# Three and six token tiles instead of four and five, 52 and 44 hosted expert groups, another order in the joint attention stage, and weights laid out by slice

## What is computed

```
a = rmsnorm(h, norm_mix)
z = a @ w_in                                  # 1024 x 9240
y_m = sigmoid(o) * mlstm_chunkwise(...)       # 4 heads of 256, a recurrent state
y_f = fox_attention(...)                      # 16 heads of 64, causal, with forget gates
h = h + (sig(g_m) * (y_m @ w_br_m) + sig(g_f) * (y_f @ w_br_f)) @ w_out
# PEER: 8 heads pick 16 experts each of 16384, by two top-16 lists of 128 keys
act = gelu(einsum('thkd,td->thk', u_tab[idx], x))
h = h + einsum('thk,thkd->td', g * act, v_tab[idx])
h = h + sigmoid(rmsnorm(h) @ w_ple_gate) * (p @ w_ple_proj)
```

## Time and profile before

| what | value |
|---|---|
| time, median of three runs | 5291.07 us (5285.33 to 5294.82) |
| the profiled execution's own time | 5289.55 us |
| its span | 5287.7 us |
| mean granted TensorE clock | 0.905 of full speed |
| TensorE, VectorE, ScalarE, GpSimd busy | 86%, 58%, 18%, 23% of the span |
| DMA | 1478.71 MB, mean 280 GB/s |

### The profile page before, as it was taken

One profiled execution on the slowest core, in us unless ns is written; L12 is line 12 of the kernel. 1 busy time (PEld: TensorE's weight loads), 2 busy tenths in 40 slices (PEclk: granted clock), 3 DMA queues, 4 the chain that ended last, 5 costly groups with the idle time before them and its releaser, 6 DMA issues. The chain is left out here.

```text
span 5287.7 us, 47730 instructions
## 1 busy us (share of the span) xinstructions
PE 4532.9 (86%) x16510; PEld 2777.6 (53%) x16510; DVE 3088.6 (58%) x6265; ACT 965.1 (18%) x1797; POOL 1233.2 (23%) x970
## 2 busy tenths in 40 slices
PE   8999669979859999677787689946899999999989
PEld 5555445536535555356566455635455445545444
DVE  1000333214567677489888617589677777777742
ACT  1110321111100111144444311113100000000013
POOL 0000001200004444243343100000344444444410
PEclk9999878889979999777776699969999999999999
DMA  4332344467729999888888687735899999999951
GB/s 143 124 113 87 103 132 152 166 232 285 255 111 392 408 407 402 315 329 317 308 332 313 243 318 276 250 122 171 355 419 419 418 414 417 412 414 415 408 233 58
DMA packets 464418, 1478.71 MB, mean 280 GB/s; under 512 B 38146, under 2 KB 204850, under 8 KB 361298
## 3 DMA queue, kind: packets, MB, share of 16 engines
q0 software_dynamic: 119872, 824.76, 38.7%
q1 hardware_dynamic: 344338, 651.36, 34.3%
HBM read 1370.05 MB, written 115.38 MB: 281 GB/s over the span
## 5 line engine op out<-in xcount | busy, mean ns | idle before, releaser
L2252 POOL DMA_INDIRECT ex_uv<-in_uv,idx x768 | 1142.2, 1487 | 1898.0 <-DVE ex_acc L2309 1646.0
L2293 DVE CUSTOM_DVE_ANT_0 ex_uv<-ex_uv,ex_xp 128x1024 f32<-128x1024 f32 x768 | 915.4, 1221 | 350.3 <-DMA ex_uv<-in_uv,idx 304.7
L2309 DVE SCALAR_TENSOR_TENSOR ex_acc<-ex_uv,ex_wt,ex_acc 128x1024 f32<-128x1024 f32 x768 | 942.2, 1280 | 6.3
L2599 PE MATMUL exp_psum_dn<-exp_dn_big,exp_dn_gg 128*128 128x512 f32 x1536 | 683.4, 595 | 28.1 <-DVE exp_dn_gg L2521 28.1
L2590 PE MATMUL exp_psum_dn<-exp_dn_xT,exp_dn_big 128*128 128x384 f32 x2048 | 684.0, 488 | 13.3 <-DMA exp_dn_big<-in_ud 13.3
L386 PE MATMUL proj_psum_acc<-proj_w,aT_later 128*128 128x385 f32 x1920 | 624.8, 487 | 71.0 <-DMA proj_w<-in_w_in 64.3
L2590 PEld LDWEIGHTS exp_psum_dn<-exp_dn_xT,exp_dn_big 128*128 128x128 f32 x2048 | 390.4, 191 | 313.3 <-issue 62.4
L386 PEld LDWEIGHTS proj_psum_acc<-proj_w,aT_later 128*128 128x128 f32 x1920 | 363.9, 190 | 331.5 <-DMA proj_w<-in_w_in 64.5
L297 PE MATMUL proj_psum_acc<-proj_w,aT 128*128 128x385 f32 x1536 | 501.7, 488 | 5.0 <-DVE aT L230 2.8
L2599 PEld LDWEIGHTS exp_psum_dn<-exp_dn_big,exp_dn_gg 128*128 128x128 f32 x1536 | 290.4, 190 | 377.5 <-issue 350.8
L297 PEld LDWEIGHTS proj_psum_acc<-proj_w,aT 128*128 128x128 f32 x1536 | 291.0, 190 | 211.8 <-issue 4.4
(11 more groups left out here) (363 smaller groups left out, 4560.4 us busy)
## 6 DMA issues: line engine op xcount, KB each, us to landing
proj_w<-in_w_in SPq DMA_DIRECT2D x48, 1540.0 KB, 36.3
rt_w<-in_w_q SPq DMA_DIRECT2D x36, 2048.0 KB, 8.2
exp_dn_big<-in_ud SPq DMA_DIRECT2D x128, 512.0 KB
exp_dn_big<-in_vd SPq DMA_DIRECT2D x128, 512.0 KB, 8.1
scratch_z<-proj_zs SPq DMA_DIRECT2D x216, 192.5 KB, 2.2
rt_w<-in_w_br_m SPq DMA_DIRECT2D x18, 2048.0 KB, 10.0
rt_w<-in_w_br_f SPq DMA_DIRECT2D x18, 2048.0 KB
rt_w<-in_w_out SPq DMA_DIRECT2D x18, 2048.0 KB, 8.9
```

What stands on the lines that cost most here:

```text
L2252: pool.indirect_dma_start(self.uv[:, slot, :], None, self.uv_tab, bass.IndirectOffsetOnAxis(ap=self.idx[:, at:at + 1], axis=0)).then_inc(s ...
L2293: dve.tensor_tensor_reduce(self.uv[:, slot, 0:D], self.uv[:, slot, 0:D], self.xp[:], 1.0, 0.0, ALU.mult, ALU.add, self.dot[:, g % 2, j:j + ...
L2309: dve.scalar_tensor_tensor(out=self.acc[:, j % 2, :], in0=self.uv[:, slot, D:2 * D], scalar=self.wt[:, g % 2, j:j + 1], in1=self.acc[:, j ...
L2599: mm = pe.matmul(self.banks[t][:, n * 512:(n + 1) * 512], self.gg[:, 4 + q % 4, t * P:(t + 1) * P], self.big[:, 4 + q % 4, n * 512:(n + 1) ...
```

## The change

`FIRST` goes from 4 to 3 and `EARLY` from 44 to 52. So the front stage and the first routing handle three tiles, the first attention two blocks, and the second part handles six tiles and six blocks (3 to 8). The projection hosts 52 groups and the joint stage 44. In `stage_attend` ScalarE copies the turned probabilities of the step before ahead of the exponential, and VectorE scales the rows of the step before the last directly behind the maximum. The weights `w_in`, `w_br_m`, `w_br_f`, `w_out` and `w_q` are laid out on the host so that what one load brings stands contiguously for each partition. Some small buffers share memory.

```diff
-FIRST = 4
+FIRST = 3
 HOSTED = 3
-EARLY = 44
+EARLY = 52
...
-                sp.dma_start(w[:, u % U], w_in_v[:, :, u * CW:(u + 1) * CW]).then_inc(w_in_u[u % U], 16)
+                sp.dma_start(w[:, u % U].rearrange("p k n -> p (k n)"), w_in[u]).then_inc(w_in_u[u % U], 16)
...
-                if j + 3 * nt in rides:
+                if rides.get(j + 3 * nt, 0) >= nm.XB:
                     nm.sp_load(sp, rides[j + 3 * nt])
...
-        self.SBUFS = 1024 // self.W if self.W <= 512 else 1
+        self.SBUFS = 2 if self.W <= 512 else 1
...
                     for hd, g in fx.heads_at(s):
                         fx.act_head(act, hd, g)
-                    fx.act_exp(act, s)
                     ml.act_slot(act, *slot(s, 0))
                 if s >= 1:
                     for r in range(fx.rounds(s - 1)):
                         fx.act_probs(act, s - 1, r)
+                if s < STEPS:
+                    fx.act_exp(act, s)
                 for g, unit in hosted(s, 0):
                     ex.act_unit(act, g, unit)
...
-            for s in range(STEPS + 1):
+            for s in range(STEPS + 2):
                 if s < STEPS:
                     fx.dve_max(dve, s)
+                if s >= 2:
+                    fx.dve_y(dve, s - 2)
+                if s < STEPS:
                     ml.dve_slot(dve, *slot(s, 0))
                 for g, unit in hosted(s, 0):
                     ex.dve_unit(dve, g, unit)
                 if s < STEPS:
                     ml.dve_slot(dve, *slot(s, 1))
-                if s >= 1:
-                    fx.dve_y(dve, s - 1)
...
-        self.wD, self.A = st.sb("nwD", [P, P]), st.sb("nA", [P, P])
-        self.inter, self.num, self.kw = st.sb("ninter", [P, DA]), st.sb("nnum", [P, DA]), st.sb("nkw", [P, 2, DM])
+        self.wD, self.A = self.dx[:, 0, :], self.dM[:, 0, :]
+        self.inter, self.kw = st.sb("ninter", [P, DA]), st.sb("nkw", [P, 2, DM])
+        self.num = self.inter
...
-        picked, flat = st.sb("picked", [P, 2, PH, TOPK]), st.sb("flat", [P, EXPERTS])
+        picked, flat = partf, top[:].rearrange("p h k -> p (h k)")
...
         def branch_w(g):
-            half = slice(g // 2 * 512, g // 2 * 512 + 512)
-            return (w_br_m, w_br_f)[g % 2].rearrange("(k p) n -> p k n", p=P)[:, :, half]
+            return (w_br_m, w_br_f)[g % 2][g // 2]
...
+    slices = lambda v, width: c(v.reshape(KD, P, -1, width).transpose(2, 1, 0, 3)).reshape(-1, P, KD * width)
```

More of the change, by code:

```diff
@@ L344, in stage_project @@
         out = [st.sem(f"out{s}") for s in range(SLOTS)]
-        w_in_v = w_in.rearrange("(k p) n -> p k n", p=P)
         def hosted(j):
@@ L1764, in stage_route @@
         part, partf = st.sb("part", [P, 2, PH, TOPK], U32), st.sb("partf", [P, 2, PH, TOPK])
-        picked, flat = st.sb("picked", [P, 2, PH, TOPK]), st.sb("flat", [P, EXPERTS])
+        picked, flat = partf, top[:].rearrange("p h k -> p (h k)")
         ramp_i, ramp = st.sb("ramp_i", [P, TOPK], mybir.dt.int32), st.sb("ramp", [P, TOPK])
         ex, tot, itot = st.sb("ex", [P, PH, TOPK]), st.sb("tot", [P, PH]), st.sb("itot", [P, PH])
-        ss, ms, rt, rs = (st.sb(n, [P, 1]) for n in ("ss", "ms", "rt", "rs"))
+        stat = st.sb("stat", [P, 4])
+        ss, ms, rt, rs = (stat[:, n:n + 1] for n in range(4))
         bank = [st.ps(f"b{n}", [P, 512]) for n in range(RING)]
@@ L1799, in branch_w @@
         def branch_w(g):
-            half = slice(g // 2 * 512, g // 2 * 512 + 512)
-            return (w_br_m, w_br_f)[g % 2].rearrange("(k p) n -> p k n", p=P)[:, :, half]
+            return (w_br_m, w_br_f)[g % 2][g // 2]
         def out_w(g):
-            return w_out.rearrange("(k p) n -> p k n", p=P)[:, :, g * 512:(g + 1) * 512]
+            return w_out[g]
         def query_w(g):
-            return w_q.rearrange("(k p) n -> p k n", p=P)[:, :, g * 512:(g + 1) * 512]
+            return w_q[g]
         user = [g_branch(0, g) for g in range(4)] + [g_out(0, g) for g in range(2)]
@@ L1829, in slice_in @@
                     wait_full(sp, user[k - RING])
-                sp.dma_start(w[:, k % RING], view).then_inc(w_in[k % RING], 16)
+                sp.dma_start(w[:, k % RING].rearrange("p k n -> p (k n)"), view).then_inc(w_in[k % RING], 16)
             def tile_y(t):
@@ L2009, in root @@
                     wait_full(act, g_turn_x(t - 1, 1))
-                act.activation(xp[:], h[:], ACT.Square, accum_out=ss[:]).then_inc(squared, 1)
+                act.activation(xp[:], h[:], ACT.Square, accum_out=ss).then_inc(squared, 1)
                 act.wait_ge(meaned, t + 1)
-                act.activation(rt[:], ms[:], ACT.Sqrt).then_inc(rooted, 1)
+                act.activation(rt, ms, ACT.Sqrt).then_inc(rooted, 1)
             def turned_x(t):
@@ L2090, in mean @@
                 dve.wait_ge(squared, t + 1)
-                dve.tensor_scalar(ms[:], ss[:], 1.0 / D, EPS, ALU.mult, ALU.add).then_inc(meaned, 1)
+                dve.tensor_scalar(ms, ss, 1.0 / D, EPS, ALU.mult, ALU.add).then_inc(meaned, 1)
             def normed(t):
                 dve.wait_ge(rooted, t + 1)
-                dve.reciprocal(rs[:], rt[:]).then_inc(inverted, 1)
+                dve.reciprocal(rs, rt).then_inc(inverted, 1)
                 dve.wait_ge(inverted, t + 1)
-                dve.scalar_tensor_tensor(out=xp[:], in0=h[:], scalar=rs[:], in1=gb[:], op0=ALU.mult, op1=ALU.mult
+                dve.scalar_tensor_tensor(out=xp[:], in0=h[:], scalar=rs, in1=gb[:], op0=ALU.mult, op1=ALU.mult
                                          ).then_inc(xp_set, 1)
@@ L2165, in numbers @@
                 step(t, 15, dve.tensor_reduce(tot[:], ex[:], AX.X, ALU.add))
-                dve.scalar_tensor_tensor(out=flat[:], in0=picked[:, 0].rearrange("p h k -> p (h k)"),
+                dve.scalar_tensor_tensor(out=flat, in0=picked[:, 0].rearrange("p h k -> p (h k)"),
                                          scalar=float(PKEYS), in1=picked[:, 1].rearrange("p h k -> p (h k)"),
@@ L2170, in numbers @@
                 at = slice((t0 + t) * EXPERTS, (t0 + t + 1) * EXPERTS)
-                dve.tensor_copy(idx[:, at], flat[:])
+                dve.tensor_copy(idx[:, at], flat)
                 step(t, 17, dve.tensor_tensor(gate[:, at].rearrange("p (h k) -> p h k", h=PH), ex[:],
@@ L2918 @@
         pT=c(np.concatenate([I["p_sample"].reshape(NSEQ * DSEQ, -1), I["p_prompt"].reshape(SEQ, -1)]).T),
-        norm_mix=cols(I["norm_mix"]), w_in=I["w_in"][0],
+        norm_mix=cols(I["norm_mix"]), w_in=slices(I["w_in"][0], CW),
         gate_bias=np.concatenate([I["mlstm_b_i"], I["mlstm_b_f"], I["fox_b_f"]], axis=1),
@@ L2925 @@
         n0=c(I["state_mlstm_n"][0].reshape(NSEQ, H_M, 2, P).transpose(3, 0, 1, 2).reshape(P, -1)),
-        w_br_m=I["w_br_m"][0], w_br_f=I["w_br_f"][0], w_out=I["w_out"][0],
-        norm_ffn=I["norm_ffn"], w_q=I["peer_w_q"][0],
+        w_br_m=slices(I["w_br_m"][0], 512), w_br_f=slices(I["w_br_f"][0], 512), w_out=slices(I["w_out"][0], 512),
+        norm_ffn=I["norm_ffn"], w_q=slices(I["peer_w_q"][0], 512),
         keys=c(np.stack([I["peer_keys1"][0], I["peer_keys2"][0]], axis=1).reshape(2 * PH, PKEYS, P).transpose(2, 0, 1)),
```

1 line of the change is left out of this document (removed).

## The result

The changed kernel takes 5152.98 us (median of 4 runs, 5148.67 to 5157.32), the kernel before 5289.83 (4 runs, 5285.33 to 5294.82; the table of the time before has the median of three). The ratio is 0.9741, with a 95% interval of 0.9724 to 0.9758: 137 us less, where 141 were forecast. The profiled execution took 5157.32 us, 4.3 above its median, with a span of 5155.3.

A forecast was written before the change was run, and what follows sets the result against it. TensorE was taken to bound the projections; in the joint stage VectorE (88% full) and a slow TensorE held each other up. First attention -73, joint stage -64, layout -4 sum to -141: 5149 us, range 5095 to 5225.

The forecast's parts named there:

- Tiles: Projections and routing: 24 steps move from front stage to second projection, -125 and +125 us; one routing tile moves, net 0.
- First attention: First attention, three blocks to two: 95 us busy plus 18 us waiting gives 113 against 186, -73 us (bounds -61, -91).
- Groups: Second projection, 44 to 52 hosted groups: VectorE needs 510 of 780 us, DMA load falls from 98% to 95%, cost 0.
- Joint stage: Joint stage, six blocks, 44 groups and new order: 754 us becomes 690, -64 us (bounds 664 and 723).
- its 36.5 us go: Joint stage: VectorE's `dve_y` scales the step before the last, so its 36.5 us of waits for the mix disappear.
- its check of TensorE's side: Joint stage: TensorE needs 465 us at full clock; with 58 us of waits, 713 us at 0.71 or 639 at 0.80.
- The bound of 723 us: Joint stage, upper bound: VectorE's busy 614 us plus the old idle share, 91/80 us a step, in all 96 steps.
- Layout: Weights laid out by slice: half of two 4.36 us waits at routing stages' first matmuls saved, -4 us (bounds 0, -9).
- The clock and VectorE's floor: Joint stage: shorter waits keep the clock near 0.89, stage at 664 us or below, total 5123 us; chance 0.13.
- The wait moves to the exponential: Joint stage: next scores wait for a later exponential, about 7.9 us a step, stage 760, total 5219 us; chance 0.15.
- The step keeps its length: Joint stage: three-engine round trip keeps maxima 9.5 us apart, 96 steps take 905 us, total 5364 us; chance 0.04.
- The copies of the second projection starve: Second projection: longer weight packets delay gathers, Gelu and copies, 6 us in each of 29 rounds, total 5323 us; chance 0.02.

## Why the prediction was right, point by point

**Tiles.** Right. 24 projection steps and one tile of routing moved across at equal price: +117.7 and +90.4 against -131.9 and -93.2. Each part of the projection pair came out 7 us better than its 125: in the second the waits for ScalarE's copies, 6.7 us, are gone; in the front 4.1 are a shorter wait for the first attention block's rows (20.4 instead of 24.5), and 1.7 an earlier first matmul (12.8 instead of 14.5), nearly all of it a shorter wait for ScalarE's normalised rows (8.7 instead of 10.3). Other runs with the same front stage start at 13.0 to 14.1, so that much is spread. I had put all of these at 0.

**First attention.** -75.3 against -73, from two terms that were off in opposite senses: TensorE is busy 85.6 us, not 95, and the wait for the copy is 14.4, not 18, but the stall behind the mLSTM loads, 7.2 us, was not foreseen. It shows in the order of SyncE's queue, where the prediction had not looked for the shorter stage.

**Groups.** Right in what it costs, and in kind in what it gives. VectorE spent 504.87 us in the projection (52 x 9.8 = 510 forecast). The joint stage was to lose 8 x 9.8 = 78 us of VectorE's work; between the runs with 44 and 52 groups it lost 72.5, of which 59 came through as time. The DMA engines had the room that the sum showed: 0.96 of the window against 1.00 before, and 56 groups still fitted.

**Joint stage.** The mis-sized term. The prediction gave 690 by "VectorE 614, other waits 39, without work 11, and a Gelu that is 26 us later". VectorE's busy time is 617.84, the Gelu wait 38.0 us, below the 51 of the sum. But the waits that "stay" did not: the maximum's wait for scores is 48.0 us and not 13.7. The step that failed is "its 36.5 us go": they went, but the scaling, put behind the maximum, is late for the next mix, TensorE loses 39.6 us on it, its scores are late, and so is VectorE's next maximum. The swap of the two lines takes 24 us off the stage in the traces (711.1 to 687.6) and 17 off the kernel; the run with the old layout, in which nothing of this stage was edited, has 701.2, so a part of the 24 can be spread. The path was wrong as well. The sum let the order gain through VectorE's waits for the mix; but with ScalarE's half alone 24.7 us of them are left and the stage is as short, and VectorE's half alone makes it longer. The gain runs through TensorE's wait for the copy, which the prediction had named as the trouble but had only in its check of TensorE's side. That side held: 471 us at full clock against 465 forecast, and the clock 0.78 lies in the 0.75 to 0.85 named.

The old order with six tiles was mis-sized too. The bound of 723 us held the old idle share per step fixed; measured were 761.4 between the maxima. So the sum gave the order 723 - 690 = 33 us of the joint stage and it brought 50; it had the tiles and groups take 754 - 723 = 31 us off and they added 10. The first error made up 17 us of the 41 of the second, and 24 were left. The prediction had not asked what each part is worth alone.

**The total.** That 137 us came out where 141 were forecast is partly luck. The joint stage gained 24 us less than forecast, the layout 4 less, and the stretch ahead of the first joint maximum came out 4 longer. Against that the projection pair gained 14 us that the sum did not have, the stretch with the samples 4, and the first attention, the gate stages and the routing 5 together; and the profiled execution, which the ledger is taken from, lay 4 us above its median. Three small slips of the sum change nothing: 5146.7 + 1.9 + 1.5 is 5150 and not 5149; the lower end of the main case's own range leaves out the layout's 9 us and would be 5100; and the 905 us of the unchanged step are 96 x 754/80, not 96 x 9.5.

**Layout.** -4 forecast, 0 measured with 52 groups. The waits of 4.36 us at the first matmul became 3.77: half a microsecond each. What the layout gives is about 10 us once the DMA engines are full, by one pair of runs whose intervals overlap.

**The rivals.** "The clock and VectorE's floor" (5123) is what the swap (5136) and 56 groups (5131) come near to from two sides, each with a clock of 0.80 to 0.81; it needed edits that the change did not have. The prediction had also priced the stage at 523 us near full clock. With the hosted work taken out it went there, to 0.94 and 542 us; with it in, the clock stayed at 0.78. The rule behind that price is the Trainium skill's ("TensorE: Matmul & The Clock Gate", on what is actually happening), that activity releases the throttle, and the traces agree with it in kind. "The wait moves to the exponential" (5219) happened in kind, 34.1 us in 34 waits, far below the 150.6 of the wait that it was to replace. "The step keeps its length" is refuted by 7.5 us a step and by 5.6 without hosted work. "The copies of the second projection starve" did not happen: ScalarE's wait for z rows, 206.2 us before, has no row after. The weights' long packets pushed the gathers back by 1 us at most: with 56 groups these landed after 12.9 us with the old layout and 13.9 with the new, while the weights went from 31.7 to 12.9. The Trainium skill ("DMA: Bandwidth & Descriptors", on queues and rings) has each DMA engine take turns between its queues, packet by packet. The two landings fit that; no run here shows the turns themselves.

## What to carry to other kernels

Where engines work through lists in order, look for the result that another engine waits for and put it ahead of what nobody waits for yet: ScalarE's copies ahead of the exponential were worth all 62 us of the order, and VectorE's scaling ahead of the maximum 17 more. When a consumer is moved later to spare its own wait, ask who needs the buffer it frees. Move background work to where the bound engine leaves room, and count that room in bytes as well as in engine time: here it was full at 56 groups, and the four next ones cost 25 us.

## What the runs showed of the hardware

What the DMA engines can move depended on the packets of a minor part of the bytes. The middle 500 us of the second projection, first with 60 groups and the new layout, then with 56 and the new one, then with 56 and the old one:

```profile
1300.00:1800.00 500.00, 500.00 (x1545) 292.05 (x1544) 387.85 (x516) 46.66 (x138) 237.19 (x157) 1.00 1.02 421
```

```profile
1300.00:1800.00 500.00, 500.00 (x1545) 292.07 (x1544) 376.75 (x503) 52.72 (x136) 238.19 (x156) 1.00 1.01 418
```

```profile
1300.00:1800.00 500.00, 496.40 (x1528) 289.70 (x1527) 370.35 (x494) 49.98 (x133) 229.09 (x152) 1.00 1.02 408
```

With the same groups and nearly the same share, 1.01 and 1.02, the old layout moved 408 GB/s against 418, 2.4% less. 421 GB/s is also what the run with 64 groups moved there. A price per MB that was taken where the share was 0.98 overstated the need by 4% (39.4 engine-us per MB, against 38.0 by 16 engines and 421 GB/s).

The product of TensorE's busy time and granted clock stayed between 461 and 474 us in eleven runs of the same 96 joint steps, and was 451 in the one without hosted work, while its busy time went from 479 to 623 us, so a share of busy time says little without the clock beside it. And a wait taken away came back as clock: in the two runs without the one stall the first attention had 0.97, in the eight that share the copies' new place and have a stall of 4.5 to 7.6 us it had 0.89 to 0.93.
